# Weight panels converted in two halves by ScalarE, with TensorE and GpSimd waiting for each half

## The reference

```python
# layer 0: h += hgrn2_mixer(rmsnorm(h)); h += swiglu_ffn(rmsnorm(h))
# layer 1: h += dilated_attention_mixer(rmsnorm(h)); h += swiglu_ffn(rmsnorm(h)); h = rmsnorm(h)
# hybrid layer: z = rmsnorm(x) @ w_in            (7 x 1024 columns: recurrence, convolution, gates)
#   x += merged @ w_out; x += (silu(g) * u) @ w_down; x += sigmoid(rmsnorm(x) @ w_ple_gate) * (p @ w_ple)
def swiglu_ffn(u, w_in, w_down):                 # three of them, inner width 2816
    gate, up = jnp.split(u @ w_in, 2, axis=-1)
    return (jax.nn.silu(gate) * up) @ w_down
```

## Time and profile before

| | us |
|---|---|
| median of 3 executions (2283.93, 2284.17, 2291.8) | 2284.17 |
| the profiled execution: its own time | 2282.93 |
| its span, from the first to the last instruction | 2281.2 |
| TensorE busy (96% of the span) | 2181.2 |
| GpSimd busy (48%) | 1085.0 |
| VectorE busy (41%) | 942.3 |
| ScalarE busy (35%) | 805.8 |
| ScalarE, 187 conversions of a panel | 356.7 |
| mean granted clock of TensorE | 0.981 of full |

### The profile page before, as it was taken

How to read it: one execution, slowest core, us unless ns; L and a number is a source line. 1 busy time by engine, 2 the same in 40 slices (tenths; PEclk the granted TensorE clock), 3 DMA queues, 4 the chain that set the end, 5 groups by cost and what they waited for, 6 DMA issues and landing times.

```text
span 2281.2 us, 26008 instructions
## 1 busy us (share of the span) xinstructions
PE 2181.2 (96%) x9850; PEld 1805.8 (79%) x9850; DVE 942.3 (41%) x1258; ACT 805.8 (35%) x880; POOL 1085.0 (48%) x817
## 2 busy tenths in 40 slices
PE   7999989999999999999999999879999899999996
PEld 5888867888888778977888888668887678888875
DVE  6255644223122356443322223874567642231224
ACT  5223344223223344544322232313555432232232
POOL 4465425444554433335444455535554454445554
PEclk9999999999999999999999999989999899999998
DMA  4211102222232222113222233222222222222321
GB/s 164 75 61 51 55 23 107 92 98 104 92 111 101 93 74 74 62 68 117 105 92 92 95 108 110 74 74 92 92 92 87 79 93 92 102 101 92 111 102 56
DMA packets 30198, 203.16 MB, mean 89 GB/s; under 512 B 3252, under 2 KB 3508, under 8 KB 6200
## 3 DMA queue, kind: packets, MB, share of 16 engines
q1 hardware_dynamic: 30136, 202.29, 25.0%
HBM read 200.18 MB, written 2.10 MB: 89 GB/s over the span
## 4 chain that ended last, share of the span: by engine, by line
PE 82%; DVE 11%; ACT 4%; issue 3%; POOL 0%; DMA 0%; DVEq 0%; ACTq 0%; SPq 0%; POOLq 0%
PE bank L1443 81%; DVE x L1332 1%; DVE ssq L962 1%; ACT L584 1%; ACT w_hi L584 1%; ACT rstd L584 1%; DVE aqk L1203 1%; DVE x L1395 1%; DVE m_hi L1407 0%; DVE h L971 0%; DVE h L1342 0%; DVE un L946 0%; POOL ssq L570 0%; ACT s_a L584 0%; DVE un L1201 0%
## 5 line engine op out<-in xcount | busy, mean ns | idle before, releaser
L496 POOL TENSOR_TENSOR w_lo<-raw,w_hi 128x512 fp32r<-128x512 f32 x680 | 928.0, 1394 | 1028.5 <-ACT w_hi L584 1028.5
L1443 PE MATMUL bank<-u_hi,w_hi 128*128 128x512 f32 x1952 | 770.7, 395 | 34.4 <-DVE u_lo L950 15.1
L1443 PE MATMUL bank<-u_lo,w_hi 128*128 128x512 f32 x1952 | 763.2, 391 | 0.0
L1443 PE MATMUL bank<-u_hi,w_lo 128*128 128x512 f32 x1952 | 494.2, 393 | 0.0
L584 ACT ACTIVATE w_hi<-raw 128x2048 fp32r<-128x2048 f32 x187 | 356.7, 1907 | 299.5 <-PE bank L1443 295.0
L1443 PEld LDWEIGHTS bank<-u_hi,w_hi 128*128 128x128 f32 x1952 | 368.8, 189 | 116.4 <-issue 20.9
L1443 PEld LDWEIGHTS bank<-u_hi,w_lo 128*128 128x128 f32 x1952 | 369.6, 189 | 80.7 <-issue 3.4
L1443 PEld LDWEIGHTS bank<-u_lo,w_hi 128*128 128x128 f32 x1952 | 368.9, 189 | 76.8 <-issue 1.4
L994 DVE TENSOR_TENSOR sq<-bank,rstd 128x512 f32<-128x512 f32 x66 | 45.6, 692 | 480.1 <-PE bank L1443 480.1
L584 ACT ACTIVATE sq<-sq 128x512 f32<-128x512 f32 x82 | 51.7, 631 | 538.4 <-DVE sq L994 495.1
L1443 PE MATMUL bank<-act_hi,w_hi 128*128 128x512 f32 x528 | 205.4, 389 | 0.0
(11 more groups left out here) (237 smaller groups left out, 2165.1 us busy)
## 6 DMA issues: line engine op xcount, KB each, us to landing
raw<-wall SPq DMA_DIRECT2D x187, 1024.0 KB, 4.8
h<-x_t SPq DMA_DIRECT2D x4, 512.0 KB, 7.7
out_t<-h SPq DMA_DIRECT2D x2, 512.0 KB, 2.8
out_t<-h SPq DMA_DIRECT2D x4, 256.0 KB, 3.0
lmask_f<-lmask_in SPq DMA_DIRECT2D x1, 512.0 KB
cs<-cs_in SPq DMA_DIRECT2D x1, 512.0 KB, 3.5
pf<-p_t SPq DMA_DIRECT2D x1, 512.0 KB, 3.5
amask<-amask_in SPq DMA_DIRECT2D x1, 256.0 KB
```

Of the source, the lines that this page charges most:

```text
L496: ins = nc.gpsimd.tensor_tensor(w_lo[:, s, c], raw[:, s, c], w_hi[:, s, c].bitcast(F32), ALU.subtract)
L1443: return nc.tensor.matmul(out, lhsT, rhs, start=start, stop=stop, skip_group_check=True)
```

## The change

ScalarE converts a panel by two ACTIVATEs of 1024 columns. The first signals a new semaphore `half_ready`, the second `hi_ready`. GpSimd waits for `half_ready` before its first two subtractions and for `hi_ready` before the other two. TensorE, in `panel` alone, waits for `half_ready` before its first matmul and for `hi_ready` before the fifth row block. `by_tokens`, `k_step` and the gate and "ple" panels are as before. Nothing else is moved.

```diff
@@ def lo(p, s, i=None)        # GpSimd, in loops
-                pool.wait_ge(hi_ready, q + 1)
                 for k in range(PANEL // S):
+                    if k % 2 == 0:
+                        pool.wait_ge(hi_ready if k else half_ready, q + 1)
@@ def lo_piece(p, a, b)       # GpSimd, first mixer
-                if a == 0:
-                    pool.wait_ge(hi_ready, p + 1)
                 for k in range(a, b):
+                    if k % 2 == 0:
+                        pool.wait_ge(hi_ready if k else half_ready, p + 1)
@@ def conv(p, i=None, step=2) # ScalarE
-                af(w_hi[:, s, :], raw[:, s, :], ACT.Copy).then_inc(hi_ready, 1)
+                af(w_hi[:, s, 0:PANEL // 2], raw[:, s, 0:PANEL // 2], ACT.Copy).then_inc(half_ready, 1)
+                af(w_hi[:, s, PANEL // 2:PANEL], raw[:, s, PANEL // 2:PANEL], ACT.Copy).then_inc(hi_ready, 1)
@@ def panel(...)              # TensorE
-                pe.wait_ge(hi_ready, at(p + 1, i, pstep))
+                pe.wait_ge(half_ready, at(p + 1, i, pstep))
                 if first:
                     pe.wait_ge(group_free, at(g + 1, i, gstep))
                 for n, k in enumerate(ks):
+                    if n == 4:
+                        pe.wait_ge(hi_ready, at(p + 1, i, pstep))
```

More of the change, by code:

```diff
@@ L260, in build @@
         out_stored = sem("out_stored")
+        half_ready = sem("half_ready")
         hi_ready = sem("hi_ready")
```

## The result

The changed kernel takes 2292.08 us (median of 20 executions, 2284.82 to 2297.03) against 2283.86 of before (20 executions, 2279.72 to 2291.8): ratio 1.003, 95% interval 1.0021 to 1.0039. It is 8 us slower, in the range (2281 to 2296), under 0.5%, and more than the 3 us that the sum gave. By the means it is 7.5 us (2292.08 against 2284.56). In a second comparison, five rounds, it was 2290.47 against 2284.26, ratio 1.0025 (1.0012 to 1.0039).

A forecast was written before the change was run, and what follows sets the result against it. TensorE holds 82% of the chain of waits, VectorE 11%; where the chain leaves TensorE, VectorE's durations depend on GpSimd. The terms sum to +3.0 us on 2282.93, 2285.9, or 2287.2 as median; range 2281 to 2296.

The forecast's parts named there:

- start: Kernel start: GpSimd starts earlier, so three of its instructions meet VectorE and not four; -0.7 us.
- panel 18: The one TensorE wait for w_hi on the path: TensorE resumes 0.84 us earlier; -0.8 us.
- norms 1, 2, 3, 5, 6: GpSimd's second instruction starts 0.16 us ahead of ssq, so TensorE waits 0.4 us longer at each; +2.0 us.
- norm 4: Norm with four additions: the fourth now finds GpSimd done; -0.5 us.
- end of a0, panels 2 to 4 of a1: GpSimd starts just ahead of L1202, delaying VectorE's chain by 0.84 us at each of four places; +3.4 us.
- rx: First rx panel, the same case as the start: GpSimd's first instruction falls beside reads of PSUM; -0.7 us.
- yg: Eight-iteration loop: L1406 held up in place of the scan, nearly nothing per iteration, +0.86 in the last; together +0.5 us.
- rival A: yg loop: the scan takes 2.11 us by itself, so every iteration pays; +6.4 us more, 2293.6; chance 0.12.
- Rival B: Norms: VectorE comes ahead of GpSimd's second instruction; 5 x (-1.0) us, 2282.2; chance 0.15.
- Rival C: Fifth row block of 162 panels: TensorE pays for the added wait; +16 us, 2303; chance 0.04.
- Rival D: TensorE's five w_hi waits each lose 0.84 us and collisions even out; -4.2 us, 2280; chance 0.05.
- rival E: Longer stalls at three norms let TensorE's clock fall to 1.2 GHz; up to +8.5 us, 2295.7; chance 0.08.

The follow-up runs named there:

- E0: The changed kernel measured once more, nothing altered: 2290.47 us, ratio 1.0025 to before.
- E3: Against E1, GpSimd begins on the first half while TensorE still waits for the whole conversion: 2291.42 us, ratio 1.0027 to before.
- E1: Against before, only ScalarE's conversion is split in two; TensorE and GpSimd both still wait for the whole: 2283.11 us, ratio 0.9986.
- E2: Against E1, TensorE begins on the first half with its added wait; GpSimd still waits for the whole: 2280.94 us, ratio 0.9976 to before.
- E4: Against the changed kernel, GpSimd waits for the whole conversion in seven panels, end of a0 to a2's second: 2281.72 us, ratio 0.9974 to before.
- E5: Against E2, GpSimd at the six norms subtracts only after VectorE's last addition to ssq: 2269.72 us, ratio 0.9915 to before.
- E7: E5 and E6 together, GpSimd on halves only for panels 0 and rx+2, panel cx+2 waiting for scaled h: 2247.42 us, ratio 0.9813 to before.
- E6: Against E2, GpSimd in the yg loop subtracts while VectorE waits for the gelu: 2270.11 us, ratio 0.9923 to before.

## Why the prediction was right, and where it fell short

The sum, term by term, in shifts of TensorE's matmuls between the two traces:

| step | forecast | measured |
|---|---|---|
| start | -0.7 | -0.76, of which 0.2 is lost again in the first mixer |
| panel 18 | -0.8 | -1.1 |
| norms 1, 2, 3, 5, 6 | +2.0 | +0.54, and four times +0.38: +2.1 |
| norm 4 | -0.5 | -0.49 |
| end of a0, panels 2 to 4 of a1 | +3.4 | +0.83, +0.84, +0.86, +0.81: +3.3 |
| first a1 panel | -0.2 | -0.14 |
| rx | -0.7 | -1.0 (the wait at 1474.84 fell from 1.50 to 0.49), and -0.2 up to the first cx panels |
| a2, behind the rotation | 0 | +0.7 |
| yg | +0.5 | +0.9 |
| sum | +3.0 | +3.5 |

The sum left out a2: at 923.92 in the trace of the changed kernel TensorE waits 0.30 us for VectorE (`DVEq L1209`) where it had not waited in before. The wait is there in E0 and E3 too, and not in E1 and E2. The other errors are small and partly cancel.

So the mechanism is shown, not only argued: who starts first goes through, the other waits. Its trace signs are those forecast (`ssq` at 4.23, L1205 and L1409 held up, the scan at 1.23 us), E3 against E1 puts the loss on GpSimd's start, and E4 finds 3.3 us of it in seven panels. The chosen reading of the scan, from the factor of two, was right; rival A is out, and the rule of the Trainium skill that I set beside it ("SBUF — State Buffer", Who interferes with whom) agrees: 1.23 us alone, 2.11 against GpSimd. The yg term was a little small because the gain per iteration did not appear: an iteration takes the same 13.1 us. The margins are another matter. In a1 the order before hung on 0.04 us, and the prediction, which took 0.10 us for the longer conversion, did not ask what the split alone would do there; E1 shows that it turns the order round, for 4.4 us.

Rival B is out: `ssq` came 0.16 to 0.18 us behind GpSimd's second instruction at all six norms. Rival C is out by the step of the weight loads and by E2; so is the estimate of 8 to 16 us from the Trainium skill ("Advanced Engine Details and Errata", section Network/Comms): a wait that is already satisfied is not paid here. Rival D is out: three of TensorE's four waits for `w_hi` in the yg loop stayed, the first fell from 1.70 to 0.85 us, and the wait for `m_lo` behind the loop grew from 8.2 to 9.9.

What the sum lacked is the rest of the 8 us. It is of the kind of rival E, the clock, which I had priced at three norms; behind the norms TensorE's time at the lower level stayed within about half a microsecond. Of the 12 us between the two traces 8.5 are clock: they lay behind the lengthened stalls at 778 and 874 us (1.6 and 0.8 us in the first trace; the second trace has only the latter, E3 neither) and in the attention's output projection (about 6.5 us). The term that fell short is the clock, which the sum put at nothing. Comparing at equal clock gives 3.7 us, close to the sum. That the forecast range held the result is owed in part to rivals A and E, which had widened it for other places.

Open: whether the change lowers the clock, or only happened to meet it lower. The long form of the output projection stands in the traces of the changed kernel (twice), E1, E3, E4, E5 and E7, the short one in before, E2 and E6, so it does not go with GpSimd's early start; and one profile per kernel cannot tell how often each has it. The averages over all executions (0.9784 and 0.9792 against 0.9798) are apart by about the spread of their own repeats. So the 3.7 us are shown as the cost of the order, and the rest of the 8 us is only accounted for by the clock; its cause is not shown.

## What to carry to other kernels

Starting a helper engine earlier is not free when it and the engine on the critical path hold each other up, as GpSimd and VectorE do here: list which instructions of the two meet before and after the shift, since each meeting costs the other engine up to 1.1 us here (the helper's own instruction takes 1.29), and a shift of less than 0.1 us can decide one. The larger gain was in the opposite direction, letting GpSimd wait until VectorE's chain has passed; it had the slack for it, but for 1.8 us of TensorE's waits. And where executions of one kernel differ by its granted clock, compare at equal clock before explaining a few microseconds.

## What the runs showed of the hardware

- A GpSimd tensor_tensor that reads SBUF and a VectorE instruction with two SBUF inputs hold each other up: `aqk` takes 0.69 us alone and 1.79 beside GpSimd. A cast on SBUF is held up too (`m_hi`: 0.43 us in E6, 1.31 in before). A held VectorE tensor_tensor of 512 columns ends 0.54 us after the GpSimd one; an instruction with PSUM and one SBUF input was not touched (L1218 in before's second a1 panel took 0.69 us at 829.61, while GpSimd was busy from 825.32 to 830.81).
- `tensor_tensor_scan` of 512 columns takes 1.23 us alone and 2.11 held up. Held up it ends 1.08 us after GpSimd's instruction, twice the 0.54 of a tensor_tensor, and alone it takes 0.54 more than a tensor_tensor's 0.69.
- Two ScalarE conversions of 1024 columns back to back take 1.99 us, one of 2048 takes 1.90: the split costs 0.09 us, not the 0.21 that the single durations add up to.
- A conversion that ends 0.09 us later (E1) took 1.10 us off the path at each of four places; by the whole times that is 1.2 us by the medians and 3 at equal clock. I had not expected that a delay could be a gain at that scale.
